# Moving the normed activations from 64 to 192 bytes modulo 512 in SBUF, in a two-layer encoder kernel

## The chip, the cores and the metric

The kernel runs on one core of a Trainium2 chip. The metric is the device time of one execution in microseconds (us), the median of several executions. Matrix products run on TensorE (PE in the profile, its weight loads PEld), elementwise work on VectorE (DVE) and ScalarE (ACT), some loads are issued by GpSimd (POOL), and the stream of weights by SyncE (SP).

## What is computed

Two layers of an encoder over 512 tokens of width 1024, in float32. Cut to what matters here:

```python
for l in range(2):
    x = x + 0.5 * rms_norm(swiglu(rms_norm(x, g0), w_in[l, 0], w_out[l, 0]), g1)
    u = rms_norm(x, g2); proj = u @ w_in_mix[l]            # 24 column blocks of 128
    y = concat(norm(neighbourhood(proj_a)), norm(hyena(proj_b)), norm(dilated(proj_c)))
    x = x + rms_norm(y @ w_out_mix[l], g4)
    x = x + rms_norm(cross_attention(rms_norm(x, g5), rms_norm(mem, g6)), g7)
    x = x + 0.5 * rms_norm(swiglu(rms_norm(x, g8), w_in[l, 1], w_out[l, 1]), g9)
# swiglu(h, a, b): gate, up = split(h @ a); (silu(gate) * up) @ b, hidden width 2816
```

## The kernel before

**Products.** Each float32 matrix is split in two parts of the type fp32r, a high one (`wh`, `uH`, ...) and a low one (`wl`, `uL`, ...), and each product is three matmuls one behind the other: high by high, high by low, low by high. A matmul names a stationary operand (128 columns, loaded into the array by a weight load that runs beside the matmul before it) and a moving operand (256 or 512 columns that stream through).

**Tiles.** `uH` and `uL` hold the normed, transposed activations of the sub-layer at work, as [128, 8, 512]; the mixer's and the cross attention's results are put there too. `wh` and `wl` are rings of four weight tiles, 128x1024 each. A shared region behind `uH` and `uL` is laid out again for each stage: `hs` (the hidden activations, split), `T1H` to `T4L` (sums of quarters of the activations), `memH`/`memL`, `qXh`, `kXh` and others.

**Stages.** Four feed-forward stages, two in each layer. Each begins with `first_units` (L456 to L458: weights stationary, half of `uH`/`uL` moving, 256 columns). Then 20 times `group`, which forms 7 products of 4 x 3 matmuls (`factor_product`, L504 to L506: weights stationary, 256 columns moving): three of the seven take `uH`/`uL` as the moving operand, four take `T1` to `T4`. Their order in a group is u, u, T2, T1, T3, u, T4. Then `out_units` (through `products`, L399 to L403) with `hs` stationary and the weights moving, 512 columns. Between the feed-forward stages lie the mixer and the cross attention: projections by `unit` (through `products` as well: weights stationary, `uH`/`uL` moving, 512 columns), attention, and an output product with `uH`/`uL` stationary and weights moving, 512 columns. The keys of the memory are projected with `memH`/`memL` moving at 256 columns, its values with `memH`/`memL` stationary and the weights moving at 512.

**Order.** Each engine's program is written out by hand; semaphores tie them. The stages' waits on PE are for split weights (`split_ready`, `low_a` and the like), for activations (`u_ready`) and for free PSUM banks.

**Addresses.** Tensors are allocated in the order of the code, one behind the other. Counted per partition, `wh` and `wl` begin at 128 bytes modulo 512, `uH` and `uL` at 64 (byte 105536 and byte 121920), and so does everything in the shared region that the products above read (it begins at byte 138304). All slices that the products take of them begin at multiples of 512 bytes from there, so a tile's residue is that of every operand cut from it. Counting pieces of 64 bytes modulo 512, `uH`, `uL` and the region start seven pieces behind the weights, which is the same as one piece ahead of them. The residue is set by one pad:

```python
pr = sb("pr", [P, NPAR + ALIGN])     # ALIGN = 106 float32 of padding
```

It stands ahead of `negmax`, `den`, `rden`, `gss`, `qCh`/`gain_rows`, `uH`, `uL` and the region, in this order.

Of the kernel before, what the change touches and what calls it, by code (L numbers as in the profile page):

```python
# [13 lines left out]
P = 128  # L14
# [54 lines left out]

G0, CW0, CB0, SK0, NPAR = 0, 80, 98, 104, 106  # L70

ALIGN = 106
PRE = (0, 2, 5, 8)
POST = (1, 4, 7, 9)
G_GROUP, G_MEM = 3, 6
# [4 lines left out]
def build(nc, x, mem, par, grow, w_first, w_second, w_proj, rpb, t5, fw1, fw23, fw4, fvec, decay,  # L80
          k_emb, k_fwd, k_inv, k_time, k_namask, k_hot, k_lnn, k_eye, out):
    with ExitStack() as ctx:
        def sb(name, shape, dt=F32):
            return ctx.enter_context(nc.sbuf_tensor(name, shape, dt))
# [22 lines left out]
        epsc = sb("epsc", [P, 2])  # L107
        pr = sb("pr", [P, NPAR + ALIGN])
        negmax = sb("negmax", [P, ITEMS])
# [5 lines left out]
        def place(parts):  # L115

            made = {}
            with ExitStack() as st:
                for name, shape, dt in parts:
                    made[name] = st.enter_context(nc.sbuf_tensor(name, shape, dt))  # L120
            return made
# [4 lines left out]
        g_post, g_pre = gain_rows[:, 0:D], gain_rows[:, D:2 * D]  # L126
        uH = sb("uH", [P, DT, T], F32R)
        uL = sb("uL", [P, DT, T], F32R)
        fact = place([("hid", [P, FT * T], F32), ("T2H", [P, 4, HALF], F32R), ("T2L", [P, 4, HALF], F32R),
                      ("T1H", [P, 4, HALF], F32R), ("T1L", [P, 4, HALF], F32R),  # L130
                      ("T3H", [P, 4, HALF], F32R), ("T3L", [P, 4, HALF], F32R),
# [1923 lines left out]
```

## Time and profile before

| what | us |
|---|---|
| median of 3 executions | 2318.16 |
| lowest and highest | 2312.68, 2326.12 |
| the profiled execution | 2327.44 |
| its span, first to last instruction | 2325.6 |

The page gives busy time by engine, the span in 40 slices, and the chain of work that ended last. A matmul's duration on the page is modelled and overlaps with the next one's, so the rate of TensorE is read from start to start, in the timeline, or from the number of matmuls in a stretch, not from the mean duration. A count of a stretch takes in the matmuls that its edges cut, some two too many.

### The profile page before, as it was taken

The numbers are of one execution on the slowest core, as the hardware profiler recorded it, in microseconds if no ns is written. First come the engines' busy times: TensorE is split into PE (matmuls) and PEld (weight loads), VectorE is DVE, ScalarE is ACT, GpSimd is POOL, SyncE is SP. The second block draws the span as 40 slices with busy tenths as digits, with TensorE's granted clock in tenths as the row PEclk, the third lists the DMA queues.
The fourth block names the chain that finished last, engine by engine and source line by source line (L and its number), as shares of the span: only waits on it lengthen the run. The fifth ranks groups of instructions, "written<-read, shape, count | busy, mean of one in ns | idle before, by whom it ended". The sixth has DMA issues, their size and how long they took to land.

```text
span 2325.6 us, 38259 instructions
## 1 busy us (share of the span) xinstructions
PE 2295.1 (99%) x15046; PEld 2056.9 (88%) x15046; DVE 1577.4 (68%) x2191; ACT 1064.5 (46%) x1765; POOL 109.3 (5%) x185
## 2 busy tenths in 40 slices
PE   7999999999999999999999999999999999999998
PEld 7999888777888899998899998887778888999987
DVE  7999437645365499994399993476464654999833
ACT  5445335227454364443364443352284544644522
POOL 0000000610000000000000000007000000000000
PEclk9999999999999999999999999999999999999999
DMA  4333323240234133323233333232402341333332
GB/s 140 110 113 123 117 82 136 73 142 25 73 110 145 55 110 109 108 99 109 82 111 108 108 102 110 79 136 73 147 19 73 118 145 46 113 115 108 117 92 81
DMA packets 66225, 236.00 MB, mean 101 GB/s; under 512 B 8882, under 2 KB 10632, under 8 KB 65600
## 3 DMA queue, kind: packets, MB, share of 16 engines
q1 hardware_dynamic: 57600, 209.74, 27.1%
q0 software_dynamic: 8224, 24.12, 3.2%
q8 instruction: 77, 1.26, 0.2%
q10 hardware_dynamic: 288, 0.59, 0.1%
q14 instruction: 36, 0.29, 0.0%
HBM read 232.29 MB, written 2.12 MB: 101 GB/s over the span
## 4 chain that ended last, share of the span: by engine, by line
PE 95%; ACT 2%; DVE 2%; issue 1%; DMA 1%; DVEq 0%; SPq 0%; ACTq 0%
PE bank L399 14%; PE bank L403 14%; PE bank L401 14%; PE bank L506 11%; PE bank L504 11%; PE bank L505 11%; PE bank L653 4%; PE bank L456 2%; PE bank L458 2%; PE bank L457 2%; PE bank L628 2%; PE bank L724 1%; PE bank L441 1%; PE bank L613 1%; PE bank L589 1%
## 5 line engine op out<-in xcount | busy, mean ns | idle before, releaser
L313 DVE TENSOR_TENSOR wl<-raw,wh 128x1024 fp32r<-128x1024 f32 x232 | 301.9, 1301 | 371.9 <-ACT wh L308 371.2
L308 ACT ACTIVATE wh<-raw 128x1024 fp32r<-128x1024 f32 x232 | 245.0, 1056 | 492.5 <-PE bank L403 412.1
L399 PE MATMUL bank<-wh,hs 128*128 128x512 f32 x704 | 278.5, 396 | 0.0
L403 PE MATMUL bank<-wh,hs 128*128 128x512 f32 x704 | 276.1, 392 | 0.0
L401 PE MATMUL bank<-wl,hs 128*128 128x512 f32 x704 | 273.6, 389 | 0.0
L504 PE MATMUL bank<-uH,wh 128*128 128x256 f32 x960 | 268.0, 279 | 0.0
L506 PE MATMUL bank<-uH,wl 128*128 128x256 f32 x960 | 267.8, 279 | 0.0
L505 PE MATMUL bank<-uL,wh 128*128 128x256 f32 x960 | 267.8, 279 | 0.0
L1367 DVE TENSOR_TENSOR wl<-S,wh 128x1024 fp32r<-128x1024 f32 x160 | 194.5, 1216 | 0.0
L506 PEld LDWEIGHTS bank<-uH,wl 128*128 128x128 f32 x960 | 181.3, 189 | 0.0
L505 PEld LDWEIGHTS bank<-uL,wh 128*128 128x128 f32 x960 | 181.3, 189 | 0.0
L504 PEld LDWEIGHTS bank<-uH,wh 128*128 128x128 f32 x960 | 180.3, 188 | 0.9 <-issue 0.9
L403 PEld LDWEIGHTS bank<-wh,hs 128*128 128x128 f32 x704 | 132.2, 188 | 30.8
L401 PEld LDWEIGHTS bank<-wl,hs 128*128 128x128 f32 x704 | 132.2, 188 | 28.8
L399 PEld LDWEIGHTS bank<-wh,hs 128*128 128x128 f32 x704 | 132.6, 188 | 27.1 <-issue 1.3
L951 ACT ACTIVATE wh<-S 128x1024 fp32r<-128x1024 f32 x80 | 85.2, 1065 | 154.6 <-DVE S L1355 121.0
L399 PE MATMUL bank<-uH,wh 128*128 128x512 f32 x384 | 154.0, 401 | 0.0
L401 PE MATMUL bank<-uL,wh 128*128 128x512 f32 x384 | 151.7, 395 | 0.0
L403 PE MATMUL bank<-uH,wl 128*128 128x512 f32 x384 | 151.6, 395 | 0.0
L456 PE MATMUL bank<-uH,wh 128*128 128x256 f32 x512 | 146.6, 286 | 4.2 <-DVE uL L1282 4.1
L458 PE MATMUL bank<-uH,wl 128*128 128x256 f32 x512 | 143.9, 281 | 0.0
L457 PE MATMUL bank<-uL,wh 128*128 128x256 f32 x512 | 143.9, 281 | 0.0
(273 smaller groups left out, 5866.3 us busy)
## 6 DMA issues: line engine op xcount, KB each, us to landing
raw<-in_w_proj SPq DMA_DIRECT2D x128, 512.0 KB, 3.5
raw<-in_w_first SPq DMA_DIRECT2D x96, 512.0 KB, 3.6
raw<-in_w_second SPq DMA_DIRECT2D x88, 512.0 KB, 3.4
side<-in_w_first SPq DMA_DIRECT2D x40, 512.0 KB, 3.5
raw_value<-in_w_first SPq DMA_DIRECT2D x40, 512.0 KB, 4.2
gain_rows<-in_grow POOLq DMA_DIRECT2D x15, 512.0 KB, 5.2
strip<-bias_of_distance POOLq DMA_DIRECT2D x2, 2688.0 KB, 13.7
strip<-in_rpb POOLq DMA_DIRECT2D x96, 24.0 KB, 2.2
```

What stands on the lines that cost most here:

```text
L308: e.activation(wh[u % RING][:], raw[u % RAWS][:], ACT.Copy).then_inc(high_ready, 1)
L313: e.tensor_tensor(wl[u % RING][:], raw[u % RAWS][:], wh[u % RING][:].bitcast(F32), ALU.subtract).then_inc(split_ready, 1)
L399: e.matmul(b[:, c], still_h, hi[:, c], start=first and c.start == 0, stop=False)
L401: e.matmul(b[:, c], still_h, lo[:, c], start=False, stop=False)
L403: mm = e.matmul(b[:, c], still_l, hi[:, c], start=False, stop=last and c.stop == n)
L456: e.matmul(bank[j][:, n], wh[u % RING][:, w], uH[:, k, n], start=half + k == 0, stop=False)
L457: e.matmul(bank[j][:, n], wh[u % RING][:, w], uL[:, k, n], start=False, stop=False)
L458: mm = e.matmul(bank[j][:, n], wl[u % RING][:, w], uH[:, k, n], start=False, stop=half == 1 and k == DT - 1)
L504: e.matmul(to, still_h, bH[:, k, :], start=k == 0, stop=False)
L505: e.matmul(to, still_h, bL[:, k, :], start=False, stop=False)
L506: mm = e.matmul(to, still_l, bH[:, k, :], start=False, stop=k == 3)
L1367: e.tensor_tensor(block_of(wl, base, n)[:, 0:cols], source, block_of(wh, base, n)[:, 0:cols].bitcast(F32), ALU.subtract).then_inc(low_done, 1)
```

## The change

Of the padding in front of `negmax`, 96 float32 (384 bytes per partition) are taken out and put in as a tensor of its own, `back`, behind `uL`. So `negmax`, `den`, `rden`, `gss`, `qCh`/`gain_rows`, `uH` and `uL` move down by 384 bytes, and the region and everything in it stays. `uH` and `uL` now begin at 192 bytes modulo 512 (105152 and 121536), one piece of 64 bytes behind the weights' 128; the region stays at 64. No instruction is added, removed or moved on any engine; only addresses differ.

```diff
-ALIGN = 106
+ALIGN, BACK = 10, 96
...
         uH = sb("uH", [P, DT, T], F32R)
         uL = sb("uL", [P, DT, T], F32R)
+        back = sb("back", [P, BACK])
         fact = place([("hid", [P, FT * T], F32), ("T2H", [P, 4, HALF], F32R), ("T2L", [P, 4, HALF], F32R),
```

## Rows read from the trace of the kernel before

**Rows 1.** The page: span, busy time by engine, granted TensorE clock.

```profile
span 2325.6 us, 38259 instructions
PE 2295.1 (99%) x15046; PEld 2056.9 (88%) x15046; DVE 1577.4 (68%) x2191; ACT 1064.5 (46%) x1765; POOL 109.3 (5%) x185
PEclk9999999999999999999999999999999999999999
```

**Rows 2.** The page: the chain that ended last, shares by engine.

```profile
PE 95%; ACT 2%; DVE 2%; issue 1%; DMA 1%; DVEq 0%; SPq 0%; ACTq 0%
```

**Rows 3.** Groups by form: line engine op, out<-in, shapes, count | busy us, mean ns.

```profile
L504 PE MATMUL bank<-uH,wh 128*128 128x256 f32 x960 | 268.0, 279 | 0.0
...
L399 PE MATMUL bank<-uH,wh 128*128 128x512 f32 x384 | 154.0, 401 | 0.0
...
L456 PE MATMUL bank<-uH,wh 128*128 128x256 f32 x512 | 146.6, 286 | 4.2 <-DVE uL L1282 4.1 <-DVE wl L313 0.2
...
L399 PE MATMUL bank<-wh,uH 128*128 128x512 f32 x256 | 102.2, 399 | 0.0
...
L504 PE MATMUL bank<-T2H,wh 128*128 128x256 f32 x320 | 89.3, 279 | 0.0
```

**Rows 4.** Groups' stretches: length, busy us and count (PE PEld DVE ACT POOL), clock, DMA.

```profile
66.00:226.00 160.00, 160.00 (x1414) 160.00 (x1413) 156.87 (x221) 77.47 (x101) 1.71 (x4) 1.00 0.31 112
880.00:1040.00 160.00, 160.00 (x1361) 160.00 (x1360) 152.51 (x211) 74.63 (x98) 0.00 (x0) 1.00 0.30 105
1226.00:1386.00 160.00, 160.00 (x1361) 160.00 (x1360) 152.50 (x211) 74.99 (x99) 0.00 (x0) 1.00 0.30 105
2030.00:2190.00 160.00, 160.00 (x1415) 160.00 (x1414) 158.21 (x223) 78.02 (x104) 0.00 (x0) 1.00 0.32 112
```

**Rows 5.** Timeline (start, us, what), 512 columns, u moving: first and 13th matmul.

```profile
469.65 0.40 PE L403 MATMUL bank<-uH,wl 128*128 128x512 f32 x1
...
472.45 0.39 PE L403 MATMUL bank<-uH,wl 128*128 128x512 f32 x1
```

**Rows 6.** hs stationary, weights moving: timeline (first, 13th matmul), then a 100 us stretch.

```profile
299.68 0.39 PE L401 MATMUL bank<-wl,hs 128*128 128x512 f32 x1
...
302.42 0.39 PE L401 MATMUL bank<-wl,hs 128*128 128x512 f32 x1
...
245.00:345.00 100.00, 100.00 (x439) 82.11 (x438) 33.57 (x36) 29.49 (x40) 0.00 (x0) 1.00 0.30 94
```

**Rows 7.** Timeline, 512 columns, u stationary, weights moving: first and 13th matmul.

```profile
619.67 0.39 PE L403 MATMUL bank<-wh,uL 128*128 128x512 f32 x1
...
622.41 0.39 PE L403 MATMUL bank<-wh,uL 128*128 128x512 f32 x1
```

**Rows 8.** Timeline, 512 columns, memH/memL stationary, weights moving: first and 13th.

```profile
729.71 0.40 PE L403 MATMUL bank<-wh,memL 128*128 128x512 f32 x1
...
732.51 0.40 PE L403 MATMUL bank<-wh,memL 128*128 128x512 f32 x1
```

**Rows 9.** Timeline, cross attention scores, both operands from the region: five starts.

```profile
749.57 0.28 PE L589 MATMUL bank<-kXl,qXh 128*128 128x256 f32 x1
749.69 0.28 PE L589 MATMUL bank<-kXh,qXl 128*128 128x256 f32 x1
749.81 0.28 PE L589 MATMUL bank<-kXh,qXh 128*128 128x256 f32 x1
749.92 0.28 PE L589 MATMUL bank<-kXl,qXh 128*128 128x256 f32 x1
750.04 0.28 PE L589 MATMUL bank<-kXh,qXl 128*128 128x256 f32 x1
```

**Rows 10.** Groups by form on DVE: one operation, inputs from different residues.

```profile
L1367 DVE TENSOR_TENSOR wl<-S,wh 128x1024 fp32r<-128x1024 f32 x160 | 194.5, 1216 | 0.0
...
L1367 DVE TENSOR_TENSOR wl<-raw,wh 128x1024 fp32r<-128x1024 f32 x40 | 48.8, 1220 | 0.0
...
L1282 DVE TENSOR_TENSOR uL<-bank,uH 128x1024 fp32r<-128x1024 f32 x32 | 39.1, 1222 | 23.2 <-ACT uH L891 23.2
```

## The prediction, made before the changed kernel ran

> **What bounds the kernel now.** I read the page first: TensorE is busy 99% of the span and its granted clock is full in all slices [rows 1], and the chain of work that ended last is TensorE's own for 95% [rows 2]. So the question is the rate at which one matmul follows another. The page's mean durations don't tell it, since the ends are modelled. I took it from the starts in the timeline and from counts in stretches.
>
> At the full clock of 2.4 GHz a matmul of 512 columns streams in 213.3 ns and one of 256 in 106.7 ns. What is measured is more, and it is not one number. With `uH`/`uL` moving and the weights stationary, 12 steps of 512 columns take 472.45 - 469.65 = 2.80 us, 233.3 ns each [rows 5]. With `hs` stationary and the weights moving it is 2.74 / 12 = 228.3 ns, or, more exactly from 439 less 2 matmuls in 100 us, 228.8 [rows 6]; with `uH`/`uL` stationary it is 228.3 again [rows 7]. With `memH` stationary and the weights moving one stage runs at 2.80 / 12 = 233.3 ns [rows 8], though its residues are those of rows 6.
>
> At 256 columns there are two levels as well. The four feed-forward stages run the same code on the same addresses, yet in 160 us the first and the last get through 1414 and 1415 matmuls and the two in the middle through 1361 each [rows 4]. Less the two that the edges add, that is 160 / 1412 = 113.3 ns against 160 / 1359 = 117.7 ns. The step is 4.4 to 4.5 ns in both sizes. So TensorE sits on a ladder whose rungs lie 4.4 ns apart, and a stage keeps its rung for long: 160 us at one rate come out only so. The rung is not set by the address residues alone, but it may depend on them.
>
> The rung shows in the spread of times. A feed-forward stage has 20 groups of 84 matmuls, 1680; one rung higher costs it 1680 x 4.4 = 7.4 us. The profiled execution has two such stages and took 2327.4 us, 9.3 more than the median. I therefore read the median as an execution with about one stage on the upper rung, and the lowest (2312.7) as one with none. The prediction is made for the median, by what the change does to an execution with one such stage; worked against the profiled one, which has two, every saving on the upper rung would count twice.
>
> **Two walls beside it.** In the lower state VectorE is busy 156.87 and 158.21 of 160 us [rows 4]. A feed-forward stage can thus not become faster by more than 1 to 2%, whatever TensorE does: VectorE would be next. That caps the gain from a still lower rung. Outside the feed-forward stages the projections have no such wall.
>
> **The change part by part.** No instruction is added or moved. What changes is the residue of `uH` and `uL` modulo 512, from 64 to 192, against 128 of the weights.
>
> (a) Projections, `uH`/`uL` moving at 512 columns: 3 x 384 = 1152 matmuls [rows 3], all at 233.3 [rows 5]. Before, the moving operand starts one piece of 64 bytes below the stationary one; after, one piece above. The nearest rows for "one piece above" are the output products, where the weights (128) move past a stationary operand at 64: 228.3 to 228.8 [rows 6, 7]. I take that value: -4.4 x 1152 = -5.1 us. Bounds: the same amount the other way (+5.1), if the role of a tile and not the difference counts, and -10.1 for two rungs.
>
> (b) Output products of mixer and cross attention, `uH`/`uL` stationary: 3 x 256 = 768 matmuls [rows 3], at 228.3 to 228.8 [rows 6, 7]. They become "one piece below", the present state of (a), 233.3. I take +4.4 x 768 = +3.4 us; bounds 0 and +3.4, and by the other reading of the role -3.4.
>
> (c) The start of each sub-layer, `uH`/`uL` moving at 256 columns: 3 x 512 = 1536 matmuls [rows 3]. Of those, I estimate that some 300 stand on the upper rung in an execution with one slow stage (one or two of the eight starts of a sub-layer, 192 each). No row shows "one piece above" at 256 columns. The neighbours are "one piece below", 113.3 or 117.7 [rows 4], and "no difference", the attention scores with both operands at 64: (750.04 - 749.57) / 4 = 117.5 ns [rows 9]. I take the lower one, because at 512 columns "one piece above" is one rung under "one piece below" [rows 5 to 7]: -300 x 4.4 = -1.3 us. Bounds: all on the upper rung, +1236 x 4.4 = +5.4 us; one rung below the lowest, some -6.8 - 1.3 = -8.1 us.
>
> (d) The feed-forward groups. Three of the seven products move `uH`/`uL`: 3 x 960 = 2880 matmuls, 720 in each stage; the other four move `T1` to `T4`, 3840 [rows 3], whose residues stay. By the same choice as in (c), the 720 of the one slow stage come down: -720 x 4.4 = -3.2 us, while the T products keep the rung they have. Bounds: upwards the 2160 of the three fast stages at the upper rung, +9.5 us; if the T products are carried with them, 3 x 1680 x 4.4 = +22.2 us. Downwards VectorE's wall, 2% of four stages of 1680 x 113.3 = 190 us, -15 us, with the slow stage's -7.4 on top.
>
> (e) Borders. Within a group the residue of the moving operand now changes four times (u to T2, T3 to u, u to T4, T4 to the next u): 320 borders in all. No row shows such a border. I take one rung for one matmul each as the upper bound, 320 x 4.4 = 1.4 us, and zero for the sum, as after a change between tiles of equal residue nothing is seen.
>
> (f) VectorE, ScalarE and the loads that touch the moved tiles (`uL`, `uH`, `gain_rows`, `negmax` and others). The same operation takes 1216 ns from a tile at 64 and 1220 from one at 128 [rows 10]; 4 ns on the 32 writes of `uL` at 1222 is 0.1 us. I take nothing, with 1 us either way for the bound. It lies beside TensorE's work apart from the sub-layers' borders.
>
> Sum: -5.1 + 3.4 - 1.3 - 3.2 = -6.2 us, so 2318.2 - 6.2 = 2312.0 us. For the profiled execution with its two slow stages the same terms give some 4.5 us more of gain.
>
> The Trainium skill speaks against any effect here. On the page "TensorE: Matmul & The Clock Gate", section "Part 2: What happens when you issue a matmul", it says that TensorE has two independent SBUF read ports, and that loading the next weights takes no bandwidth from the running matmul. By that rule terms (a) to (e) are all zero and the time is the median of before. The trace agrees only in part: the same shape runs at 228 and at 233 ns. Part 1 of the page measures N / 2.4 GHz plus some 2.5 ns as the warm interval, 215.7 at 512 columns; no stretch of these products here comes that low.
>
> **Rivals.**
>
> *Nothing changes (2318).* The rung is chosen by how a stage happens to start, and residues have no part in it. For it: four stages with equal addresses differ [rows 4], and rows 6 and 8 have the same residues and differ. Against it: at 512 columns all projections are high [rows 5] while the output products with `hs` and `uH` are low [rows 6, 7], in both layers. The spread then stays too, 2312 to 2326.
>
 Price: (c) +5.4, (d) +9.5, (b) +3.4, (a) -5.1 or 0: +13.2 to +18.3 us, 2331 to 2336. It decides from about a quarter of the fast matmuls being affected: up to there (a) pays for it. If the T products are carried along, 12.7 more, 2345 to 2349. For it: the zero-difference row is the only neighbour on that side at this size. Against it: at 512 columns that side is the better one.
>
> *A still lower rung (2290 to 2300).* At 256 columns "one piece above" could lie one rung under "one piece below", as it does at 512, so at 109. Then the u products would save 4.4 each: (c) -8.1; in (d) 2880 x 4.4 = -12.7 and -3.2 from the slow stage, cut by VectorE's wall to some -12; (a) and (b) -1.7. Together -22, 2296 us, with VectorE busy all through the groups. For it: the analogy with 512 columns. Against it: the lowest rung seen at 256 columns in 1412 steps running is 113.3.
>
> **How the numbers follow.** Chances: the forecast 0.42, nothing changes 0.18, the upper rung 0.22, the lower rung 0.18. The predicted time is 2312.0. The range has to hold most of the two outer cases: 2295 takes in the lower rung, 2337 the upper one without the carried T products; what is left out is the carried case and a part of the tails, under 0.2. The forecast's own range, by the scatter of one stage's rung in the median, is 2304 to 2319. A difference of 0.5% (11.6 us) is about what a measurement of this kernel can tell from no change. Faster by more: the lower rung and a small part of the forecast, where the T products come down as well, 0.26. Slower by more: the upper rung, 0.23. The rest, 0.51, within it.
>
> **What would show it.** In the profile after: projections at 228.8 and not 233.3 from start to start prove (a); the output products with `uH` stationary at 233.3 prove (b), those with `hs` must stay at 228.8. In the feed-forward groups the u products have to be looked at apart from the T products: 113.3 for both is the forecast, 117.7 for u alone the slow rival, 109 the fast one, with VectorE at 159 to 160 of 160 us. If the four stages still differ among each other as before, for u and T alike, nothing changed. I would be wrong most of all if the role of a tile matters and not the difference of the residues, or if the borders inside a group throw TensorE off its rung every time.

## The result and the profile after

The changed kernel takes 2335.29 us (median of 6, 2330.84 to 2338.89) against 2318.24 us for the kernel before (median of 6, 2312.68 to 2326.12): a ratio of 1.0075, 95% interval 1.0053 to 1.0097. I had forecast 2312.0, within 2295 to 2337, as no measurable change. The time lies in the range, at its slow end; the direction was wrong. The time is that of the rival "the upper rung everywhere that u moves at 256 columns", priced at 2331 to 2336.

The page of the changed kernel, its profiled execution (2338.89 us). TensorE is as full as in [rows 1], and the span is 11.5 us longer:

```profile
span 2337.1 us, 38259 instructions
PE 2306.9 (99%) x15046; PEld 2071.1 (89%) x15046; DVE 1567.6 (67%) x2191; ACT 1065.5 (46%) x1765; POOL 115.2 (5%) x185
```

Stretches inside the groups of the four feed-forward stages of the changed kernel, to be laid beside [rows 4] (length; busy us and count on PE, PEld, DVE, ACT, POOL; granted clock, DMA):

```profile
80.00:240.00 160.00, 160.00 (x1361) 160.00 (x1361) 151.97 (x210) 75.67 (x99) 2.13 (x4) 1.00 0.31 112
880.00:1040.00 160.00, 160.00 (x1389) 160.00 (x1388) 156.25 (x219) 75.72 (x99) 0.00 (x0) 1.00 0.31 112
1226.00:1386.00 160.00, 160.00 (x1361) 160.00 (x1360) 152.87 (x213) 74.48 (x98) 0.00 (x0) 1.00 0.30 107
2030.00:2190.00 160.00, 160.00 (x1361) 160.00 (x1360) 152.94 (x212) 74.73 (x97) 0.00 (x0) 1.00 0.30 105
```

None reaches the 1414 of before. Three count 1361, and the second 1389, which lies between the two rungs. The timeline of that second stage shows why: the first matmul of T3, of the u product behind it, and of T4 behind that, 12 matmuls apart each.

```profile
901.20 0.28 PE L506 MATMUL bank<-T3H,wh 128*128 128x256 f32 x1
...
902.56 0.28 PE L506 MATMUL bank<-uH,wh 128*128 128x256 f32 x1
...
903.97 0.28 PE L506 MATMUL bank<-T4H,wh 128*128 128x256 f32 x1
```

T3 took 1.36 / 12 = 113.3 ns a matmul, u 1.41 / 12 = 117.5. In the other three stages T stands at 117.6 too, but for the first two groups of the first stage. Read from all starts of the two traces, the mean interval of the u products of the groups rose from 115.65 to 117.95 ns and that of the T products from 115.58 to 116.56.

The projections and the output products did what terms (a) and (b) said. Projections with u moving (beside [rows 5]), then output products with u stationary (beside [rows 7]), the first and the 11th matmul:

```profile
469.65 0.39 PE L403 MATMUL bank<-uL,wh 128*128 128x512 f32 x1
...
471.94 0.39 PE L405 MATMUL bank<-uH,wl 128*128 128x512 f32 x1
...
619.71 0.39 PE L405 MATMUL bank<-wh,uL 128*128 128x512 f32 x1
...
622.04 0.39 PE L401 MATMUL bank<-wh,uH 128*128 128x512 f32 x1
```

2.29 / 10 = 229 ns where it was 233.3, and 2.33 / 10 = 233 ns where it was 228.3.

The profiled executions add up, by the sums of start-to-start intervals: groups' u products +6.6 us, T products +3.8, starts of the sub-layers +2.2, keys of the memory (whose tiles did not move) +0.8, projections -4.7, output products +2.9, together 11.7 us. The rest of the kernel took 0.2 less, and the span grew by 11.5. The medians are 17 us apart, since the profiled execution of before was one with two stages on the upper rung.

### The profile page after: what moved, and what is told of

It is laid out like the page before. It is cut to its first block, busy times and chain, and to the rows that moved or that the text cites. A ratio compares the mean times of both kernels' runs of the same rounds, so it can differ in the third digit from the quotient of the medians.

```text
span 2337.1 us, 38259 instructions
## 1 busy us (share of the span) xinstructions
PE 2306.9 (99%) x15046; PEld 2071.1 (89%) x15046; DVE 1567.6 (67%) x2191; ACT 1065.5 (46%) x1765; POOL 115.2 (5%) x185
## 4 chain that ended last, share of the span: by engine, by line
PE 95%; ACT 2%; DVE 2%; issue 1%; DMA 1%; DVEq 0%; SPq 0%; ACTq 0%
PE bank L401 14%; PE bank L405 14%; PE bank L403 14%; PE bank L506 11%; PE bank L507 11%; PE bank L508 11%; PE bank L655 4%; PE bank L458 2%; PE bank L459 2%; PE bank L460 2%; PE bank L630 2%; PE bank L726 1%; PE bank L443 1%; PE bank L615 1%; PE bank L591 1%
## 5 line engine op out<-in xcount | busy, mean ns | idle before, releaser
L315 DVE TENSOR_TENSOR wl<-raw,wh 128x1024 fp32r<-128x1024 f32 x232 | 286.1, 1233 | 366.2 <-ACT wh L310 365.9
```

What stands on the lines that cost most here:

```text
L315: e.tensor_tensor(wl[u % RING][:], raw[u % RAWS][:], wh[u % RING][:].bitcast(F32), ALU.subtract).then_inc(split_ready, 1)
```

## The experiments

Each ratio is against executions of the kernel before that ran on the same chip among those of the experiment. The kernel before itself lay between 2310 and 2335 us in these, with medians from 2324.6 to 2332.0, so a time means something only beside its ratio. The same holds for the result: its 0.75% was measured beside a kernel before at 2318. Against these medians the changed kernel's 2335.3 would be only 3 to 11 us slower, but it was not run beside them.

### What the interval depends on: a kernel of matmul rows alone

The rows of `m1_residues` are made by this; `s` and `m` are tiles at chosen residues, `ROW` is 24:

```python
for k in range(ROW):
    mm = e.matmul(bank[n % 8][:, 0:cols], s[si][:, k % 4 * P:k % 4 * P + P], m[mi][:, 0:cols],
                  start=k == 0, stop=k == ROW - 1)
```

> A kernel of its own that computes nothing of the reference (it copies x to the output): TensorE alone, rows of 24 fp32r matmuls without any wait, each row with one stationary tile and one moving tile that begin at chosen residues modulo 512 (tiles sa to sh at 0, 64, ... 448 bytes; ma to mp at 0, 32, ... 480 bytes), 256 or 512 columns (some at 128 and 384). VectorE idle, ScalarE idle after the start. All rows once without a break, then again in reverse order with four plain float32 transposes ahead of each. Theory 1, the difference decides: the interval depends on (moving - stationary) modulo 512 alone; for a difference of +64 it is about 118 ns at 256 columns and 228.9 at 512, for -64 it is 113.3 or 117.8 at 256 and 233.3 at 512, for 0 it is 117.5 at 256. Theory 2, the role decides (where the weights' tile begins, or where the moving one begins): rows with the same difference differ with the stationary tile by 4.4 ns or more. Theory 3, the read streams play no part and other engines' traffic makes the rungs: all rows of a size take the same interval, near 109 at 256 and 216 at 512.

Timeline of its rows of 512 columns with the stationary tile `sc` at 128 bytes, the moving tile at 0, 64, ... 448 (start us, us, what). A row's interval is the distance to the next row's start, divided by 24:

```profile
429.31 5.76 PE L71 MATMUL bank<-ma,sc 128*128 128x512 f32 x24
434.90 5.75 PE L71 MATMUL bank<-mc,sc 128*128 128x512 f32 x24
440.49 5.64 PE L71 MATMUL bank<-me,sc 128*128 128x512 f32 x24
445.97 5.67 PE L71 MATMUL bank<-mg,sc 128*128 128x512 f32 x24
451.48 5.75 PE L71 MATMUL bank<-mi,sc 128*128 128x512 f32 x24
457.07 5.76 PE L71 MATMUL bank<-mk,sc 128*128 128x512 f32 x24
462.67 5.62 PE L71 MATMUL bank<-mm,sc 128*128 128x512 f32 x24
468.13 5.68 PE L71 MATMUL bank<-mo,sc 128*128 128x512 f32 x24
```

The tile `mc`, one piece below, takes 5.59 us; `me`, no difference, 5.48; `mg`, one piece above, 5.51; `mi`, two above, 5.59; then `mk` is like `mc` again and `mm` like `me`. The pattern repeats after four pieces: the difference counts modulo 256 bytes, not 512. The same at 256 columns:

```profile
207.46 2.88 PE L71 MATMUL bank<-mc,sc 128*128 128x256 f32 x24
210.18 3.02 PE L71 MATMUL bank<-me,sc 128*128 128x256 f32 x24
213.04 2.99 PE L71 MATMUL bank<-mg,sc 128*128 128x256 f32 x24
215.87 3.01 PE L71 MATMUL bank<-mi,sc 128*128 128x256 f32 x24
```

Here `mc` took 2.72 us (113.3 ns) and `mg` 2.83 (117.9). Inside the rows, without their first matmuls, the intervals over all eight stationary tiles are as follows (ns; the difference is moving minus stationary in bytes, modulo 256, so one piece above is +64 and one piece below is -64):

| difference | 512 columns | 256 columns | rows of 256 columns at 113.3 to 114.1 |
|---|---|---|---|
| 0 | 226.7 to 228.6 | 119.5 to 120.0 | 0 of 36 |
| +64 | 228.7 to 229.2 | 117.7 to 118.0, or 113.3 | 4 of 36 |
| +128 | 232.3 to 233.3 | 118.3 to 120.0 | 0 of 36 |
| -64 | 232.6 to 233.6 | 117.8, or 113.3 to 114.1 | 12 of 36 |

The one row at +128 that belongs to the kernel's very first matmuls is left out of the ranges. Rows of 128 columns take 111.5 to 111.8 ns at every difference. Beyond the difference and the two rungs, no row depends on the stationary tile, so the role of a tile doesn't matter, and TensorE was alone, so the rungs are not made by other engines. That settles (a) and (b) and leaves the point on which the forecast failed: at 256 columns +64 and -64 have the same two rungs, and which one a row gets is decided otherwise.

One reading in the kernel goes beyond this table. The values of the memory are products of 512 columns at +64. In the first layer they run at 233.3 ns [rows 8], and in the second layer of the same execution at 2.75 / 12 = 229 (first and 13th matmul):

```profile
1889.77 0.39 PE L399 MATMUL bank<-wh,memH 128*128 128x512 f32 x1
...
1892.52 0.39 PE L399 MATMUL bank<-wh,memH 128*128 128x512 f32 x1
```

In the changed kernel, where these tiles did not move, it is the other way round, 228.9 in the first layer and 233.3 in the second. So +64 can have two intervals at 512 columns too. No experiment looked into this.

### The whole kernel at other differences

`e1_region_too` is the changed kernel without `back`; the region moves with u, all moving operands are at +64 and `hs` stationary is at +64 too:

```diff
-        back = sb("back", [P, BACK])
```

> The changed kernel without the tensor back: the region moves down by 384 bytes too, so that uH, uL and everything in the region begin one piece of 64 bytes above the weights. Theory 1, the difference decides and T1 to T4 in the changed kernel are slow only where the u products carry them along: now all products of the groups are at about 118 ns in all four stages, the output products with hs stationary go from 228.9 to 233.3 (2112 matmuls, +9.3 us), the projections stay at 228.9; against the kernel before: groups 6720 x 118 = 793 us instead of some 769 (+24), starts +4, projections -5.1, output products +3.4 and +9.3: about 2353 us. Theory 2, it is the border between two residues inside a group that throws TensorE off its rung: without borders the groups go back to 113.3 in most stages, and the time is about 2328 us.

2351.68 us, ratio 1.0098 (1.0060 to 1.0137), as theory 1 said and with hardly any scatter in its four executions (2351.4 to 2352.3). All four stages count as the first does. The `hs` products (100 us, beside the 439 of [rows 6]) are at 233.3 ns by their starts:

```profile
75.00:235.00 160.00, 160.00 (x1361) 160.00 (x1360) 152.40 (x212) 73.92 (x98) 2.13 (x4) 1.00 0.30 107
...
250.00:350.00 100.00, 100.00 (x430) 80.20 (x429) 32.89 (x36) 27.74 (x36) 0.00 (x0) 1.00 0.30 100
```

So no border between residues is needed for the upper rung: at +64 alone this kernel ends there in every stage of its profiled execution, and the other times are the same.

`e2_u_four_pieces_on` tells 256 from 512 in the kernel itself, `e3_u_equal` takes the difference 0:

```diff
-ALIGN, BACK = 10, 96
+ALIGN, BACK = 42, 64     # e2: u at 320
+ALIGN, BACK = 58, 48     # e3: u at 384
```

> ALIGN, BACK = 42, 64: u begins three pieces above the weights (residue 320, four pieces from where it was before), the region stays. Theory 1, the difference counts modulo 256: this is the state of before again, projections 233.3 ns, output products 228.9, groups at 113.3 or 117.8 by stage, the time equal to before within the scatter of the stages' rungs (ratio 0.998 to 1.003). Theory 2, modulo 512: three pieces is a new place and the projections or the groups take another interval.

2325.07 us, ratio 0.9988 (0.9968 to 1.0009): the kernel before again. Projections are back at 233.3 ns, and stages stand at 113.3 or 117.8 as they fall. Modulo 256 holds.

> ALIGN, BACK = 58, 48: u begins four pieces above the weights (residue 384), which modulo 256 is no difference. By the first microkernel (theory 1, difference modulo 256): u products of the groups and the starts at 119.7 ns always, projections at 227 instead of 233.3 (1152, -7 us), output products at 227 instead of 228.9 (768, -1.3 us). Against a profiled before of 2327: groups' u products 2880 x 4.1 = +11.8, starts 1536 x 4.1 = +6.3, T products between 0 and +8.4: 2337 to 2345 us. If the sum is under 2327, intervals measured without the rest of the kernel do not carry over to it.

2329.59 us, ratio 1.0020 (1.0005 to 1.0036), 7 us under what I expected at the least. The projections and output products came to 226.7 ns as in the microkernel. The miss is in the groups. The u products averaged 119.0 and not 119.7 ns, and the T products 114.15, under the 115.58 of before, where I had them rise by 0 to 8 us: they saved 5.5. All four stages and all executions are alike (2328.8 to 2329.9). Behind a u product at difference 0 the first T product is at 115.1 and the others at 113.3, in every group; behind one at +64, in the changed kernel, T came down like that in one stage of four. The border acts on the rung, in either direction.

### What draws the rung

`m2_rungs` runs the kernel's three-matmul pattern with `below` (-64, as T and the former u) and `above` (+64, as the new u), started by small matmuls of varying width, then in the groups' order.

> A kernel of its own that computes nothing of the reference (it copies x to the output): TensorE in the three-matmul pattern of the kernel, 256 columns, weights tiles wh, wl at 128 bytes modulo 512, moving tiles below_h, below_l at 64 (one piece below, as T1 to T4 and as u before) and above_h, above_l at 192 (one piece above, as u after). First 48 products of 24 matmuls with 'below', each preceded by a small matmul of varying width and a transpose, then 48 with 'above'; then, four times each, 36 / 21 / 21 products of 12 in the groups' order u u T T T u T, with 'below' alone, with 'above' alone. All of it once with VectorE and ScalarE idle and once with both busy on 128x1024 tiles. Theory 1, both differences have the same two rungs (113.3 and 117.8) and the start draws one of them: 'below' lands on the lower rung in about a third of the starts (12 of 36 in the first microkernel), 'above' in about a tenth (4 of 36), and once drawn a rung stays for the whole product; the other engines' traffic changes none of it; in the mixed order the T products are at 113.3 only in a part. Theory 2, 'above' has only the upper rung and the four low rows of the first microkernel came from what ran before them: no 'above' product starts low here. Theory 3, traffic on VectorE and ScalarE knocks TensorE up: the shares of the lower rung fall in the second half.

Of 48 starts `below` took the lower rung in 15 (16 in the second half), `above` in 2 and 2. It was the same widths both times but for one of the 96: with both other engines at work nothing else changed. So here the draw follows almost wholly from how the run is started, and traffic moves it hardly at all. Theory 2 and theory 3 fall. Runs of one kind keep their rung for all 252 matmuls. Counts in 20 us: the second and the third run in the groups' order (at 346 and 376), one with `below` alone (435) and two with `above` alone (550, 580):

```profile
346.00:366.00 20.00, 20.00 (x172) 20.00 (x171) 0.00 (x0) 0.00 (x0) 0.00 (x0) 1.00 0.01 2
376.00:396.00 20.00, 20.00 (x176) 20.00 (x175) 0.00 (x0) 0.00 (x0) 0.00 (x0) 1.00 0.01 2
435.00:455.00 20.00, 20.00 (x179) 20.00 (x178) 0.00 (x0) 0.00 (x0) 0.00 (x0) 1.00 0.01 2
550.00:570.00 20.00, 20.00 (x172) 20.00 (x172) 0.00 (x0) 0.00 (x0) 0.00 (x0) 1.00 0.01 2
580.00:600.00 20.00, 20.00 (x179) 20.00 (x178) 0.00 (x0) 0.00 (x0) 0.00 (x0) 1.00 0.01 2
```

`above` alone can stay on either rung (172 or 179 in 20 us). The mixed order cannot stay on the lower one: read product by product, u is at 113.3 at most in the first two products of a run, and from the first T product on always at 117.8 or 118.1, while T settles at 113.3 (113.9 in the first product behind u) or at 117.5 to 117.8. These are the two forms of the changed kernel's stages: u up and T down in its second, both up in the rest.

`m3_kicks` puts one small plain float32 matmul alone ahead of each product of 24:

```python
for width in range(4, P + 1, 4):
    e.matmul(bank[6][:, 0:width], eye[:], eye[:, 0:width], start=True, stop=True)
    product(*where[kind], n=8)
```

> A kernel of its own that computes nothing of the reference (it copies x to the output). As in m2_rungs, but ahead of each product of 24 matmuls of 256 columns stands one plain float32 matmul alone (stationary eye, moving 4, 8, ... 128 columns of eye), for 'below' and for 'above', twice with the other engines idle and twice with them busy. Theory 1, the rung is drawn by where in time the first weight load and the first matmul of a product fall against each other: it is a fixed function of the small matmul's width, the same in all four passes, with several widths that give 113.3 for 'below' and fewer for 'above'. Theory 2, the rung that stood before carries over through a short break: the rows of a pass are all on one rung, whatever the width.

In four passes, two idle and two busy, `below` starts on the lower rung at 29, 29, 31 and 29 of the 32 widths and `above` at 31 each time. `above` misses at width 4. `below` misses at 84 each time, at 8 in three passes and at 4 in two; the very first product of the kernel, at width 4, took 207 ns a matmul and is on neither rung. So the widths are the same in all passes but for 4 and 8. Neither theory had it so one-sided, but theory 2 is out, as rows on different rungs stand side by side, and the draw can be loaded. The timeline around one of them, 32 columns wide:

```profile
37.04 0.28 PE L87 MATMUL bank<-below_h,wl 128*128 128x256 f32 x1
37.16 0.30 PE L92 MATMUL bank<-eye 128*128 128x32 f32 x2
37.30 0.37 PE L85 MATMUL bank<-below_h,wh 128*128 128x256 f32 x1
37.49 0.28 PE L86 MATMUL bank<-below_l,wh 128*128 128x256 f32 x1
37.62 0.28 PE L87 MATMUL bank<-below_h,wl 128*128 128x256 f32 x1
```

(The trace has two records for a plain float32 matmul.) From the L87 at 37.04 to that at 37.62 are three steps of the pattern, 0.58 us for what takes 3 x 113.3 = 0.34: the small matmul costs 0.24 us.

### The draw loaded in the whole kernel

The same two edits, made to the kernel before, to `e1`, to the changed kernel: TensorE's loop over groups gets a body of six groups, so that three small matmuls in a stage are enough.

```diff
+                if kick:
+                    e.matmul(bank[4][:, 0:KICK], eye[:], eye[:, 0:KICK], start=True, stop=True)
                 factor_product(base, 1, uH[:, 4:8, lo], uL[:, 4:8, lo], bank[1][:, lo])
...
-                with e.Fori(1, GROUPS_IN // 2) as it:
-                    for q in range(2):
-                        group(L, f, q, it)
+                with e.Fori(1, (GROUPS_IN - 2) // BODY + 1) as it:
+                    for q in range(BODY):
+                        group(L, f, q + 2 - BODY, it, kick=q == 0)
```

> The kernel before, with one plain float32 matmul of 20 columns (eye by eye into bank 4, which nobody reads) ahead of the second product of every sixth group, and TensorE's loop over the groups with a body of six groups instead of two: 12 such matmuls in all, some 0.2 us each. If the rung is drawn where a run of matmuls starts, and stays (theory 1), all four stages run at 113.3 ns from the first such matmul on: before has 2 to 3 stages on the upper rung at 7.4 us each, so the time is 2313 + 2.4 = about 2316 us, with hardly any scatter. If what the microkernel showed doesn't carry over (theory 2), the stages still differ from run to run and the time is that of before plus 2 us.

2317.03 us (2315.9 to 2318.8), ratio 0.9951 (0.9933 to 0.9969). The stretches of its second and fourth stage, which had both begun their first 14 products at 117.8:

```profile
880.00:1040.00 160.00, 160.00 (x1414) 160.00 (x1413) 155.84 (x216) 78.53 (x104) 0.00 (x0) 1.00 0.33 106
...
2020.00:2180.00 160.00, 160.00 (x1414) 160.00 (x1414) 157.04 (x219) 77.21 (x101) 0.00 (x0) 1.00 0.34 112
```

The control leaves the small matmuls out and keeps the loop:

```diff
-                        group(L, f, q + 2 - BODY, it, kick=q == 0)
+                        group(L, f, q + 2 - BODY, it, kick=False)
```

> e4_before_kicked without its small matmuls: TensorE's loop over the groups still has a body of six groups. If the small matmul is what starts the stages on the lower rung (theory 1), the stages differ again, 113.3 or 117.8, and the time is that of before, ratio 0.998 to 1.002, with its scatter. If it was the longer loop body (theory 2), all stages are at 113.3 and the time is 2313 to 2315 us, ratio 0.994 to 0.996.

2325.30 us, ratio 0.9999 (0.9975 to 1.0023), scattered from 2317.7 to 2325.9. Its second and third stage, one on each rung:

```profile
880.00:1040.00 160.00, 160.00 (x1413) 160.00 (x1412) 156.77 (x220) 78.83 (x104) 0.00 (x0) 1.00 0.34 109
1215.00:1375.00 160.00, 160.00 (x1361) 160.00 (x1360) 152.78 (x213) 74.41 (x98) 0.00 (x0) 1.00 0.33 108
```

So it is the small matmul, not the loop.

The kernel without small matmuls draws as well, at its own interruptions. Eight of the profiled kernels (before, `e1`, `e2`, `e4` to `e7`, `e9`) have u and T at the same difference in the groups. In their traces the rung changes 22 times inside the groups, and each time it is at a product in which a wait or a small matmul held TensorE up, with a mean interval of 121 to 126 ns. In an undisturbed stretch it never changes.

> e1_region_too (all moving operands one piece above the weights; all groups at 117.8 there, 2351.7 us) with the same 12 small matmuls and the longer loop body. Theory 1: one piece above has the same two rungs as one piece below and was only started badly; with the small matmul the groups go to 113.3 for u and T alike, 4 x 7.2 us less plus 2.4: about 2325 us. Theory 2: one piece above belongs to the upper rung in this kernel: 2354 us.

2334.95 us, ratio 1.0029 (1.0016 to 1.0043), beside 1.0098 without the small matmuls. This is 17 of the 27 us that I expected. The stages do come down, u and T alike, but in three of them only at the second small matmul, six groups late. With the groups ahead of the first small matmuls, 26 groups stay up, and 26 x 84 x 4.4 = 9.6 us is nearly all of what is missing. Here is the second stage before and after the second small matmul (117.6, then 113.3 ns):

```profile
870.00:930.00 60.00, 60.00 (x512) 60.00 (x511) 57.91 (x81) 28.73 (x37) 0.00 (x0) 1.00 0.36 118
940.00:1040.00 100.00, 100.00 (x885) 100.00 (x884) 97.93 (x137) 48.63 (x64) 0.00 (x0) 1.00 0.32 106
```

Theory 1 stands: a uniform +64 holds the lower rung in the kernel as well. Why the first small matmul misses there is open.

> The changed kernel with the same 12 small matmuls. In the microkernel's mixed order the u products went to 117.8 after the first border whatever the start, and T settled at 113.3 or at 117.5. So here u stays at 117.8 in all four stages (theory 1, the border between residues), T at 113.3 in all (3 stages x 960 x 4.2 = -12 us) or as now: 2325 us, or 2337 if T stays up. If u goes down to 113.3 as well, theory 1 is wrong about the borders and the time is about 2313.

2338.88 us, ratio 1.0042 (1.0028 to 1.0057). That is no faster than the changed kernel's 2335; the ratio is smaller because before stood higher in these runs, and the two were not run side by side. u stays at 117.7 or more in all stages; T goes from one of its two forms to the other at each small matmul but the very first, 117.6 in one block of six groups and 113.3 in the next. Here is the first stage, two blocks:

```profile
130.00:186.00 56.00, 56.00 (x479) 56.00 (x478) 53.13 (x75) 26.18 (x35) 0.00 (x0) 1.00 0.29 95
196.00:236.00 40.00, 40.00 (x349) 40.00 (x349) 38.88 (x55) 19.27 (x26) 2.13 (x4) 1.00 0.40 133
```

`e7` and `e8`, run on the same chip, name the cause together: the same small matmuls bring u down where T has the same residue, and cannot where it has another. What keeps u up in the changed kernel is the order u, T, u of unequal residues. (`e1` shows that u can also stay up without it.)

### A version that is faster than both

`e5_placed` gives each product the difference that suits it: u of the feed-forward stages stays at -64, where T is; u of mixer and cross attention sits at 0 in the same buffer; `hs` at 0.

```diff
-ALIGN = 106
+ALIGN, BACK, OVER = 122, 48, 64
...
-        uH = sb("uH", [P, DT, T], F32R)
-        uL = sb("uL", [P, DT, T], F32R)
+        both = [sb(name, [P, DT * T + OVER], F32R) for name in ("uH", "uL")]
+        uHf, uLf = (t[:, 48:48 + DT * T].rearrange("p (k n) -> p k n", k=DT) for t in both)
+        uH, uL = (t[:, 0:DT * T].rearrange("p (k n) -> p k n", k=DT) for t in both)
+        back = sb("back", [P, BACK])
...
-        hs = place([("below_hs", [P, FT * T], F32), ("hs", [P, RING, 2, T], F32R)])["hs"]
+        hs = place([("below_hs", [P, FT * T + 16], F32), ("hs", [P, RING, 2, T], F32R)])["hs"]
...
-                        e.wait_ge(factor_done, products_before(F, GROUPS_IN - 1) + (3 if j < 2 else 4))
+                        e.wait_ge(factor_done, products_before(F, GROUPS_IN - 1) + (3, 4, 4, 5)[j])
```

> The kernel before with three tiles placed by what the microkernel gave: u of the feed-forward stages stays one piece below the weights (modulo 256), u of mixer and cross attention gets no difference (the same buffer, 192 bytes lower), hs gets no difference (64 bytes higher; three of its first four writes wait for one product more). If intervals depend on the difference modulo 256 alone (theory 1): projections 226.7 instead of 233.3 (1152, -7.6 us), output products with u 226.7 instead of 228.9 (768, -1.7), those with hs 226.7 instead of 228.9 (2112, -4.6), the starts of mixer and cross attention at 120 instead of some 115.6 (768, +3.4), the groups drawing their rung as before: -10.5 us, ratio 0.9955. If the gain on the output products is lost to other waits there, -6 us or less, ratio 0.9975.

2315.72 us, ratio 0.9931 (0.9912 to 0.9951). Its `hs` products and its projections, to be laid beside the 439 of [rows 6] and beside 50 / 0.2333 = 214 of the former:

```profile
245.00:345.00 100.00, 100.00 (x443) 82.81 (x442) 34.04 (x37) 30.66 (x43) 0.00 (x0) 1.00 0.29 94
...
470.00:520.00 50.00, 50.00 (x222) 41.41 (x221) 21.64 (x23) 11.49 (x13) 0.58 (x1) 1.00 0.47 163
```

Projections and both kinds of output products run at 226.7 ns. The expected 0.9955 lies just above the interval. By the sums of intervals, against the profiled kernel before, projections and output products gave -12.3 us where I expected -13.9, and the starts took +2.0. That leaves some 6 of the 16 us; I put them down to the draw of the stages' rungs, which stood badly in the kernel before on that chip (2324 to 2333), but no trace of those executions shows it.

`e6_placed_kicked` is both edits at once.

> e5_placed (ratio 0.9931) with the same 12 small matmuls: all stages on the lower rung. 2313 - 10.5 + 2.4 = 2305 us with little scatter, against a before of 2318 to 2332: ratio 0.990 to 0.994. If VectorE, which was busy 157 of 160 us at the lower rung, holds the groups up, the count in 160 us stays under 1412 with VectorE at 160, and the gain is smaller.

2306.97 us (2304.0 to 2308.7), ratio 0.9904 (0.9885 to 0.9924): the fastest version. One of its stages:

```profile
870.00:1030.00 160.00, 160.00 (x1414) 160.00 (x1414) 157.77 (x222) 77.45 (x101) 0.00 (x0) 1.00 0.34 112
```

VectorE at 157.8 of 160 us doesn't hold it up, but there is not much left before it would.

## Why the prediction was wrong

- **What bounds the kernel.** Right: TensorE's intervals decide, in rungs of 4.4 to 4.5 ns, and the stages' rungs make the spread of times. `e4` confirms it: with all stages held low the spread shrinks from over 10 us to 3.
- **(a) and (b).** Right, in size too: -4.7 us measured for -5.1, +2.9 for +3.4. The reason, the difference and not the role, is shown by `m1_residues`.
- **(c) and (d): the step that failed.** "I take the lower one, because at 512 columns 'one piece above' is one rung under 'one piece below'". The order of two differences at 512 columns says nothing on 256. At 256 columns +64 has the same two rungs as -64; in `m2_rungs` it takes the lower one in 2 of 48 starts where -64 does in 15 or 16, and with T between at -64 it is never there behind the first T product. The row for no difference that I had [rows 9] was the nearer neighbour, and the bound made from it, all u products up, is what came: in place of -1.3 - 3.2 = -4.5 us, (c) and (d)'s u part came to +8.8 us in the profiled executions, though before already had two high stages there. The count in (c) was off as well: I took one or two of the eight starts to be on the upper rung, and in the trace of before at least four are.
- **"while the T products keep the rung they have"** in (d). Wrong as well. They rose by 1 ns on the mean (+3.8 us): behind each u product T has to come down again, and three stages of four ended in the form where it doesn't, with T at 117.6.
- **(e) Borders.** I priced them by the one matmul at the border, 1.4 us. That was the wrong kind of price; what a border does is choose the rung of the products behind it. The last sentence of the prediction named it as what would make me most wrong, and gave it no price.
- **(f)** Right: VectorE's write of `uL` takes 1222 ns on the mean before and after.
- **The rivals.** The slow one, with a chance of 0.22, had the right price, 2331 to 2336. That is in part luck: the price left out the T products, which rose. Its mechanism, one more meeting of the two read streams in every matmul, was not tested. The Trainium skill says ("TensorE: Matmul & The Clock Gate", section "Part 2: What happens when you issue a matmul") that the loading of weights takes no read bandwidth from a running matmul. I had read this as "no effect of addresses", by which all rows of a size in `m1_residues` would be equal. They differ by some 6.7 ns at 512 and at 256 columns, so the measurement decides against that reading. Whether the weight load is what costs the time, no run here isolates.

## What to carry to other kernels

Where split float32 products keep TensorE full, take the start-to-start interval of each kind of product, with the residue modulo 256 bytes of both operands beside it, before touching anything else; the mean durations hardly tell it (279 ns before and 280 to 281 after for the u products of the groups). Keep all moving operands of one back-to-back run on the same difference to their stationary ones, and measure each size by itself: the best difference was 0 at 512 columns and the worst at 256. Where equal code runs at two rates, look at how the run is started before blaming the other engines.

## What the runs showed of the hardware

- The interval of fp32r matmuls depends on the difference of the start addresses of the moving and the stationary operand modulo 256 bytes: about 226.7, 228.9, 232.4, 233.3 ns at 512 columns for 0, +64, +128, -64 once a row has settled (`m1_residues`), at the full granted clock. At half pieces, differences such as +32, it is 233 to 234. In the kernel +64 also ran at 233.3 in one layer of two ([rows 8]).
- At 256 columns and a difference of +64 or -64 there are two lasting intervals, 113.3 and 117.8 ns. In the kernels of matmuls alone, which one comes is set by the matmuls right ahead of the run, with 1 of 96 starts different once VectorE and ScalarE were at work (`m2_rungs`). In the whole kernel it differs from stage to stage and from one execution to the next.
- A single plain float32 matmul of 12 to 80 columns ahead of the run, 0.24 us, brought the lower one every time in `m3_kicks`, and in the whole kernel mostly (the first ones of three stages of `e7` did not). In the kernel before, 12 of them were worth 0.5% (`e4_before_kicked`).
- What inside the chip makes the rungs, why the period is 256 bytes, and why `e7`'s first small matmul misses, no run here shows.
